# Second-norm rows turned in 32x32 blocks on VectorE for two of four superblocks, keys turned within a projection group, and a reordered VectorE queue

## The chip, the cores and the metric

One Trainium2 chip, one of its cores. The metric is the device time of one execution in microseconds, from the runs of a kernel on the chip; the median of the runs counts. TensorE multiplies matrices and turns (transposes) tiles through the identity matrix, VectorE and ScalarE work on rows and read the banks of PSUM, POOL (GpSimd) works beside them, and SyncE (SP) issues the DMAs.

## The reference

A decoder block over 2048 tokens of width 1024, float32, then a final norm:

```python
u = rmsnorm(h, ln1_g[l])
proj = u @ w_in[l]
a_q, a_f, a_i, a_g, b_q, b_k, b_v = jnp.split(proj, SPLITS, axis=-1)
y_a = hgrn2_mixer(a_q, a_f, a_i, a_g, lower_bounds[l], hgrn_norm_g[l])
y_b = swa_sink_attention(b_q, b_k, b_v, attn_sinks[l], attn_norm_g[l])
h = h + jnp.concatenate([y_a, y_b], axis=-1) @ w_out[l]
u = rmsnorm(h, ln2_g[l])
h = h + (jax.nn.silu(u @ w_gate[l]) * (u @ w_up[l])) @ w_down[l]
```

`hgrn2_mixer` is a gated linear recurrence with 4 heads of 128 keys and values, in chunks of 64 tokens: within a chunk masked products of decayed queries and keys, between chunks a state `S = decay * S + keys^T values`, and a norm per head. `swa_sink_attention` has 8 query heads of 64 on 2 key heads, a window of 128 tokens, a linear bias and a sink. The change touches the recurrence's turned keys and states, the turned probabilities of the attention, and the second `u`.

## The kernel before

**Stages.** The tokens are taken in four superblocks of 512 (`it` = 0 to 3, four row blocks of 128 tokens each). For each the kernel computes the mixers: first norm, projection, recurrence, attention, output projection (`slots`, then `out_b`). Then the feed-forward network runs on two pairs of superblocks (`ffn`, `down`), with seven instead of eight block products. Every product of two float32 matrices is made of three products of split operands, hi and lo.

**Slots.** The order of the mixers is written out by hand: each engine has its own function `slots(it)`, which goes through slots 0 to 26. Slots 0 to 21 each begin on TensorE with a `group`: 24 products that compute 128 columns of the projection for 512 tokens. Smaller steps hang on the slots by offsets. Head `a` of the recurrence begins at slot `F_SLOT[a]`, that is 4, 9, 14 and 18. From there its forget gate, queries, values and output gate are projected in slots +0 to +3, its keys are turned and its states updated at +4 (`UPDATE`), its output is made at +5 (`OUTPUT`, which reads the states `st`), and it is normalised and turned at +5 and +6. The sixteen steps of attention run one slot apart, from slot 2 on; a step's probabilities are turned on TensorE in slots 4 to 19, two steps at a time, and VectorE brings them out of PSUM with `unfold` (line 1892).

**Units.** Slots 22 to 25 and `out_b` compute the output projection. A weight pair of 1 MB (hi and lo) is a unit, 30 to a superblock: 22 groups, four units of the first half (22 to 25), four of the second (26 to 29, in `out_b`). From superblock 1 on SyncE loads unit n with `load_split` (line 642) as soon as TensorE has done with unit n - 3, into one of three places. In `out_b` TensorE turns the next superblock's x (`prep`, line 1011): row block 0 behind unit 26, block 1 behind unit 27, blocks 2 and 3 behind unit 28. Block 1 goes to the banks M2 and M3; those are free once VectorE's `add` (line 2088) has added the output projection in them to the rows of x, which SyncE loads again with `load_rows` (line 619).

**Turned keys.** POOL writes a head's decayed keys into `kstate`, which shares memory with `forget`. `key_turn` (line 1132) turns them on TensorE into bank X3, ScalarE copies them to `kst` (line 1415), `update` on TensorE (line 1141) multiplies them with the values, and `update` on VectorE (line 1953) makes eight states in a chain. TensorE reads these in the next slot (line 1148).

**The second norm.** A superblock's rows h are squared, scaled by VectorE (line 2162) and turned while the next superblock's mixers run, in slots 18 to 25 (`UT_SLOT` = 18): step j turns half of a row block with four transposes on TensorE (`u_turn`, line 1186) into bank X0, ScalarE copies the bank to a tile `u` (`u_out`, line 1469, semaphore `s_uev`), and SyncE stores it in DRAM as `u_scr` (`store_u`, line 661, semaphores `s_us`), for `ffn` to read. The last superblock's rows are turned within `ffn`.

**SyncE's queue** is one list, in `mixers(it)`. It waits at a DMA until that DMA may go, and all behind wait too. Stores of u stand between the loads of units:

```python
for c in range(4):
    for what, n in ((("u", 3), ("r", 0), ("r", 1), ("u", 4)), (("u", 5), ("r", 2), ("u", 6)),
                    (("u", 7), ("r", 3)), ())[c]:
        if what == "u":
            store_u(it - 1, n)
        elif not last or n >= 2:
            load_rows(it, n)
    load_split(it, OUT_B + c)
```

Stores 0, 1 and 2 stand behind the loads of units 22, 23 and 24.

## Time and profile before

| | us |
|---|---|
| median of 3 runs | 2169.05 (2166.82 to 2170.37) |
| the profiled execution's own time | 2167.59 |
| its span, first to last instruction | 2165.9 |
| TensorE busy | 2134.2 (99%) |
| VectorE busy | 1364.3 (63%) |
| ScalarE busy | 843.6 (39%) |
| POOL busy | 432.5 (20%) |

The mixers take the span up to some 900 us, with superblocks 1 and 2 from 246 to 459 us and from 459 to some 676 us; the rest is the feed-forward network. A row of the trace gives line, engine, operation and tile; L1186 is line 1186 of the kernel. Durations of matrix products overlap (they are pipelined), so the chain of work, which gives each piece the time that it adds, tells better what a product costs. The engines' busy shares are of one profiled execution.

### The profile page before, as it was taken

The numbers are of one execution on the slowest core, as the hardware profiler recorded it, in microseconds if no ns is written. First come the engines' busy times: TensorE is split into PE (matmuls) and PEld (weight loads), VectorE is DVE, ScalarE is ACT, GpSimd is POOL, SyncE is SP. The second block draws the span as 40 slices with busy tenths as digits, with TensorE's granted clock in tenths as the row PEclk, the third lists the DMA queues.
The fourth block names the chain that finished last, engine by engine and source line by source line (L and its number), as shares of the span: only waits on it lengthen the run. The fifth ranks groups of instructions, "written<-read, shape, count | busy, mean of one in ns | idle before, by whom it ended". The sixth has DMA issues, their size and how long they took to land.

```text
span 2165.9 us, 28872 instructions
## 1 busy us (share of the span) xinstructions
PE 2134.2 (99%) x10708; PEld 1778.9 (82%) x10708; DVE 1364.3 (63%) x2136; ACT 843.6 (39%) x1628; POOL 432.5 (20%) x403
## 2 busy tenths in 40 slices
PE   8999999999999999999999999999999999999998
PEld 7878888888888888788888887888888888888886
DVE  5886477547754776766566765568755556564556
ACT  5343342324232423444333333356433333333445
POOL 2342022102210221222233230000222233210000
PEclk9999999999999999999999999999999999999999
DMA  7666754664467437543355657887433323237666
GB/s 247 227 231 209 264 183 145 198 223 179 146 196 229 171 132 235 217 148 115 107 209 214 218 191 234 261 267 253 172 101 102 106 89 122 93 105 236 225 208 228
DMA packets 215740, 402.48 MB, mean 186 GB/s; under 512 B 16944, under 2 KB 100912, under 8 KB 211760
## 3 DMA queue, kind: packets, MB, share of 16 engines
q1 hardware_dynamic: 215600, 400.63, 54.6%
q8 instruction: 86, 1.41, 0.3%
q14 instruction: 54, 0.44, 0.1%
HBM read 292.04 MB, written 108.53 MB: 185 GB/s over the span
## 4 chain that ended last, share of the span: by engine, by line
PE 87%; DVE 5%; issue 4%; DMA 2%; ACT 1%; POOL 1%; SPq 0%; DVEq 0%; ACTq 0%; POOLq 0%
PE M L1282 10%; PE M L1284 10%; PE M L1283 10%; PE M L971 6%; PE M L973 6%; PE M L972 6%; PE M L1307 3%; PE M L1309 3%; PE M L1308 3%; PE X L1309 3%; PE X L1308 3%; PE X L1307 3%; PE X L1284 3%; PE X L1282 3%; PE X L1283 3%
## 5 line engine op out<-in xcount | busy, mean ns | idle before, releaser
L2292 DVE TENSOR_TENSOR ring_lo<-ring_raw,ring_hi 128x1024 fp32r<-128x1024 f32 x154 | 189.7, 1232 | 162.6 <-ACT ring_hi L1707 162.1
L1707 ACT ACTIVATE ring_hi<-ring_raw 128x1024 fp32r<-128x1024 f32 x154 | 163.3, 1061 | 230.4 <-DMA ring_raw<-a_scr 225.5
L1282 PE MATMUL M<-t_hi,wu_hi 128*128 128x512 f32 x616 | 240.2, 390 | 0.3 <-DVE wu_lo L2180 0.3
L1284 PE MATMUL M<-t_hi,wu_lo 128*128 128x512 f32 x616 | 239.9, 390 | 0.0
L1283 PE MATMUL M<-t_lo,wu_hi 128*128 128x512 f32 x616 | 239.7, 389 | 0.0
L971 PE MATMUL M<-uhi,split 128*128 128x512 f32 (+1 forms) x528 | 206.6, 391 | 2.9 <-DVE ulo L1843 2.9
L973 PE MATMUL M<-uhi,split 128*128 128x512 f32 (+1 forms) x528 | 202.9, 384 | 0.0
L972 PE MATMUL M<-ulo,split 128*128 128x512 f32 (+1 forms) x528 | 202.4, 383 | 0.0
L2180 DVE TENSOR_TENSOR wu_lo<-fraw,wu_hi 128x512 fp32r<-128x512 f32 x132 | 124.0, 948 | 123.3 <-ACT wu_hi L1649 122.9
L2557 POOL TENSOR_TENSOR fs<-fraw 128x512 f32<-128x512 f32 x43 | 61.0, 1418 | 415.8 <-DMA fraw<-in_w_gate_dram 208.5
L2477 POOL TENSOR_TENSOR pr<-pr,rd 128x256 f32<-128x256 f32 x64 | 44.6, 697 | 459.1 <-DVE rd L1854 459.1
L1282 PEld LDWEIGHTS M<-t_hi,wu_hi 128*128 128x128 f32 x616 | 115.6, 188 | 25.0 <-DVE wu_lo L2180 1.1
L1283 PEld LDWEIGHTS M<-t_lo,wu_hi 128*128 128x128 f32 x616 | 115.8, 188 | 24.1
L1284 PEld LDWEIGHTS M<-t_hi,wu_lo 128*128 128x128 f32 x616 | 115.6, 188 | 24.1
L2563 POOL TENSOR_TENSOR fraw<-fraw,fs 128x512 f32<-128x512 f32 x43 | 55.9, 1300 | 369.1 <-DVE wl_lo L2180 369.1
L1307 PE MATMUL M<-ring_hi 128*128 128x512 f32 x308 | 120.4, 391 | 2.3 <-DVE ring_lo L2292 2.3
L1308 PE MATMUL M<-ring_lo,ring_hi 128*128 128x512 f32 x308 | 119.9, 389 | 0.0
L1309 PE MATMUL M<-ring_hi,ring_lo 128*128 128x512 f32 x308 | 119.9, 389 | 0.0
L1307 PE MATMUL X<-ring_hi 128*128 128x512 f32 x308 | 119.8, 389 | 0.0
L1309 PE MATMUL X<-ring_hi,ring_lo 128*128 128x512 f32 x308 | 119.8, 389 | 0.0
L1308 PE MATMUL X<-ring_lo,ring_hi 128*128 128x512 f32 x308 | 119.8, 389 | 0.0
L971 PEld LDWEIGHTS M<-uhi,split 128*128 128x128 f32 x528 | 99.3, 188 | 23.9 <-issue 5.1
(312 smaller groups left out, 5012.6 us busy)
## 6 DMA issues: line engine op xcount, KB each, us to landing
split<-w_scr SPq DMA_DIRECT2D x60, 1024.0 KB, 5.6
ring_raw<-a_scr SPq DMA_DIRECT2D x154, 256.0 KB, 3.6
w_scr<-split SPq DMA_DIRECT2D x30, 1024.0 KB, 6.5
split_next<-w_scr SPq DMA_DIRECT2D x30, 1024.0 KB, 5.0
fraw<-in_w_gate_dram SPq DMA_DIRECT2D x44, 512.0 KB, 4.8
fraw<-in_w_up_dram SPq DMA_DIRECT2D x44, 512.0 KB, 4.8
a_scr<-au SPq DMA_DIRECT2D x88, 256.0 KB, 2.4
ring_raw<-t_scr SPq DMA_DIRECT2D x88, 256.0 KB, 3.0
```

Source lines behind the costliest of these rows:

```text
L971: mm(bank, whi[s][:, kb, :], hi, start=first, stop=False)
L972: mm(bank, whi[s][:, kb, :], lo, start=False, stop=False)
L973: return mm(bank, wlo[s][:, kb, :], hi, start=False, stop=last)
L1282: mm(bank[:, :], wh[:, k, :], hi[:, k, :], start=start and k == 0, stop=False, skip_group_check=True)
L1283: mm(bank[:, :], wh[:, k, :], lo[:, k, :], start=False, stop=False, skip_group_check=True)
L1284: last = mm(bank[:, :], wl[:, k, :], hi[:, k, :], start=False, stop=k == KH - 1, skip_group_check=True)
L1307: mm(bank[:, :], hi[:, 1, tokens], hi[:, 0, :], start=first, stop=False, skip_group_check=True)
L1308: mm(bank[:, :], hi[:, 1, tokens], lo[:, 0, :], start=False, stop=False, skip_group_check=True)
L1309: done = mm(bank[:, :], lo[:, 1, tokens], hi[:, 0, :], start=False, stop=last, skip_group_check=True)
L1707: A(hi[:, :, :], raw_r[:, :, :], ACT.Copy).then_inc(s_rowhi, 1)
L2180: V.tensor_tensor(wl[:, :, :], ffn_part(p, g, o), wh[:, :, :].bitcast(F32), ALU.subtract).then_inc(s_flo, 1)
L2292: V.tensor_tensor(lo[:, :, :], raw_r[:, :, :], hi[:, :, :].bitcast(F32), ALU.subtract).then_inc(s_rowlo, 1)
```

## The change

It does five things.

- `BY_BLOCKS = 2`: for superblocks 0 and 1, VectorE turns the scaled rows (`u_blocks`): one instruction transposes every 32x32 block of a 128x512 piece in place within the tile's grid, straight from h into the tile `u`. TensorE's `u_turn` and ScalarE's `u_out` remain for superblocks 2 and 3.
- Because the blocks are turned but not moved, `store_u` places them: for those superblocks each of the eight stores becomes 16 DMAs, each of 32 partitions x 4 x 32 elements (16 KB, in pieces of 128 bytes). Counts of `s_us` follow (`u_stored`), and loads that waited for TensorE's turns wait for `s_uev`.
- `key_turn` moves from behind the group of its slot into the group, between its fourth and fifth column block, for slots 8, 13 and 18.
- VectorE's state update of head 2, in slot 18, moves ahead of the scans of head 3.
- Two unfoldings move later: the first of slot 5 to that slot's end, that of slot 13 to the end of slot 14.

```diff
@@ constants, and in block_program
+UNFOLD_LATE = (5, 13)
+BY_BLOCKS = 2
+        def u_stored(it, times):
+            parts = [16 if i < BY_BLOCKS else 1 for i in range(NSB)]
+            return 16 * (2 * sum(parts[:it]) + times * parts[it])
@@ SyncE: load_rows, store_u
-                    sp.wait_ge(s_ftr, (it - 1) * 2 * TB + 2 * b + 2)
+                    sp.wait_ge(s_uev, (it - 1) * 2 * TB + 2 * b + 2)
...
-                sp.dma_start(u_scr[it, :, 4 * half:4 * half + 4, b * P:(b + 1) * P],
-                             u_tile(it, j)[:, :].rearrange("p (c t) -> p c t", c=4)).then_inc(s_us[j % 4], 16)
+                if it >= BY_BLOCKS:
+                    sp.dma_start(u_scr[it, :, 4 * half:4 * half + 4, b * P:(b + 1) * P],
+                                 u_tile(it, j)[:, :].rearrange("p (c t) -> p c t", c=4)).then_inc(s_us[j % 4], 16)
+                    return
+                for i in range(4):
+                    tokens = slice(b * P + 32 * i, b * P + 32 * i + 32)
+                    blocks = u_tile(it, j)[32 * i:32 * i + 32, :].rearrange("c (k m t) -> c k m t", k=4, m=4)
+                    for m in range(4):
+                        sp.dma_start(u_scr[it, 32 * m:32 * m + 32, 4 * half:4 * half + 4, tokens],
+                                     blocks[:, :, m, :]).then_inc(s_us[j % 4], 16)
@@ TensorE: group, slots, out_b
-            def group(it, slot):
+            def group(it, slot, head=None):
...
                 for k in range(KD):
+                    if head is not None and k == KD // 2:
+                        key_turn(it, head)
...
-                        group(it, slot)
+                        group(it, slot, head_at(slot, UPDATE))
...
-                    a = head_at(slot, UPDATE)
-                    if a is not None and slot != OUT_A:
-                        key_turn(it, a)
...
-                    if it and 0 <= slot - UT_SLOT < 2 * TB:
+                    if it > BY_BLOCKS and 0 <= slot - UT_SLOT < 2 * TB:
                         u_turn(it - 1, slot - UT_SLOT)
...
-                        if c == 0 and bank == 0 and it:
+                        if c == 0 and bank == 0 and it > BY_BLOCKS:
                             pe.wait_ge(s_uev, it * 2 * TB)
+                        elif c == 0 and bank == 0:
+                            pe.wait_ge(s_bias, (it + 1) * STEPS)
@@ ScalarE: slots
-                    if it and 0 <= slot - UT_SLOT < 2 * TB:
+                    if it > BY_BLOCKS and 0 <= slot - UT_SLOT < 2 * TB:
                         u_out(it - 1, slot - UT_SLOT)
@@ VectorE: head_group, slots, and a new step
                     dve.wait_ge(s_f, n + 1)
+                    if a == HEADS - 1:
+                        update(it, a - 1)
...
-                        unfold(it, i)
+                        if slot not in UNFOLD_LATE:
+                            unfold(it, i)
...
-                        if a is not None:
+                        if a is not None and (step is not update or slot != F_SLOT[-1]):
                             step(it, a)
+                    for late, i in ((5, 1), (14, 9)):
+                        if slot == late:
+                            unfold(it, i)
...
+                    if 0 < it <= BY_BLOCKS and 0 <= slot - UT_SLOT < 2 * TB:
+                        u_blocks(it - 1, slot - UT_SLOT)
...
+            def u_blocks(it, j):
+                b, half = divmod(j, 2)
+                dve.wait_ge(s_u, it * TB + b + 1)
+                if j >= 4:
+                    dve.wait_ge(s_us[j % 4], u_stored(it, 1))
+                else:
+                    dve.wait_ge(s_score, (it + 1) * STEPS + STEPS)
+                V.transpose(u_tile(it, j)[:, :], h_of(it)[b][:, half * T:(half + 1) * T]).then_inc(s_uev, 1)
```

What SyncE's queue holds from the load of unit 25 to that of unit 28, in superblock 1 (`split` and `split_next` are the places of weight pairs, `h` are the rows of x). Before:

```order
L642 DMA split<-w_scr 128x2x1024
L661 DMA u_scr<-u_152 128x4x128
L619 DMA h_71<-in_x_dram 128x1024
L619 DMA h_72<-in_x_dram 128x1024
L661 DMA u_scr<-u_149 128x4x128
L642 DMA split<-w_scr 128x2x1024
L661 DMA u_scr<-u_150 128x4x128
L619 DMA h_73<-in_x_dram 128x1024
L661 DMA u_scr<-u_151 128x4x128
L642 DMA split_next<-w_scr 128x2048
L661 DMA u_scr<-u_152 128x4x128
L619 DMA h_74<-in_x_dram 128x1024
```

With the change:

```order
L649 DMA split<-w_scr 128x2x1024
L676 DMA u_scr<-u_152 32x4x32 x16
L626 DMA h_71<-in_x_dram 128x1024
L626 DMA h_72<-in_x_dram 128x1024
L676 DMA u_scr<-u_149 32x4x32 x16
L649 DMA split<-w_scr 128x2x1024
L676 DMA u_scr<-u_150 32x4x32 x16
L626 DMA h_73<-in_x_dram 128x1024
L676 DMA u_scr<-u_151 32x4x32 x16
L649 DMA split_next<-w_scr 128x2048
L676 DMA u_scr<-u_152 32x4x32 x16
L626 DMA h_74<-in_x_dram 128x1024
```

The order is the same; 80 DMAs stand where 5 stood.

VectorE in slots 18 and 19 of superblock 1 (`forget` is the forget gate, `cum` the scans, `st` the states, `u` the new transposes). Before:

```order
L1900 TENSOR_SCALAR forget<-forget,f_mul,f_add 128x512
L1907 SCALAR_TENSOR_TENSOR cum_115<-forget,ones 128x64 x8
L1953 SCALAR_TENSOR_TENSOR st_138<-state,cum_114,X 128x128
L1953 SCALAR_TENSOR_TENSOR st_138<-st_138,cum_114,X 128x128 x3
L1953 SCALAR_TENSOR_TENSOR st_139<-st_138,cum_114,X 128x128
L1953 SCALAR_TENSOR_TENSOR st_139<-st_139,cum_114,X 128x128 x3
L1892 TENSOR_TENSOR pT_136<-X,keep 128x1024
```

With the change:

```order
L1916 TENSOR_SCALAR forget<-forget,f_mul,f_add 128x512
L1971 SCALAR_TENSOR_TENSOR st_138<-state,cum_114,X 128x128
L1971 SCALAR_TENSOR_TENSOR st_138<-st_138,cum_114,X 128x128 x3
L1971 SCALAR_TENSOR_TENSOR st_139<-st_138,cum_114,X 128x128
L1971 SCALAR_TENSOR_TENSOR st_139<-st_139,cum_114,X 128x128 x3
L1925 SCALAR_TENSOR_TENSOR cum_115<-forget,ones 128x64 x8
L2182 STREAM_TRANSPOSE u_149<-h_71 128x512
L1908 TENSOR_TENSOR pT_136<-X,keep 128x1024
```

The states stand ahead of the eight scans, and the first transpose behind them.

TensorE around slot 18 of superblock 1 (`M` is the group's bank, `forget` the keys, `kst` the turned keys). Before:

```order
L971 MATMUL M<-uhi,split_next 128x512
L972 MATMUL M<-ulo,split_next 128x512
L973 MATMUL M<-uhi,split_next 128x512
L1132 MATMUL X<-ident,forget 128x128 x4
L1141 MATMUL X<-iv,kst 128x128 x8
L1186 MATMUL X<-ident,h_71 128x128 x4
L971 MATMUL M<-uhi,split 128x512
```

With the change:

```order
L986 MATMUL M<-uhi,split_next 128x512
L987 MATMUL M<-ulo,split_next 128x512
L988 MATMUL M<-uhi,split_next 128x512
L1149 MATMUL X<-ident,forget 128x128 x4
L986 MATMUL M<-uhi,split_next 128x512
L987 MATMUL M<-ulo,split_next 128x512
L988 MATMUL M<-uhi,split_next 128x512
```

The turn of the keys has products of the group on both sides, twelve before it and twelve behind.

## Rows read from the trace of the kernel before

**Rows 1.** The page: busy time and share, and the granted clock in 40 slices.

```profile
PE 2134.2 (99%) x10708; PEld 1778.9 (82%) x10708; DVE 1364.3 (63%) x2136; ACT 843.6 (39%) x1628; POOL 432.5 (20%) x403
...
PEclk9999999999999999999999999999999999999999
```

**Rows 2.** Waits of TensorE: us in total, times, longest us.

```profile
PE X L1148 <- DVE st L1953: 5.7, 5, 1.8
...
PE X L1141 <- ACT kst L1415: 2.7, 4, 0.7
```

**Rows 3.** Order of time on TensorE: start, duration, in brackets the idle time before.

```profile
128.41 1.16 PE L1148 MATMUL X<-iv,amask 128*128 128x128 f32 x8 [1.79 <-DVE st L1953]
...
160.20 0.63 PE L1132 MATMUL X<-ident,forget 128*128 128x128 f32 x4 [0.44 <-ACT iv L1409]
161.51 1.16 PE L1141 MATMUL X<-iv,kst 64*128 64x128 f32 x16 [0.69 <-ACT kst L1415]
170.22 1.16 PE L1148 MATMUL X<-iv,amask 128*128 128x128 f32 x8 [1.44 <-DVE st L1953]
...
780.23 1.16 PE L1148 MATMUL X<-iv,amask 128*128 128x128 f32 x8 [0.83 <-DVE st L1953]
```

**Rows 4.** The chain, slots 20 and 21 of superblock 1: start, us, what.

```profile
395.77 0.58 PE X L1186 x4
...
404.00 0.44 PE X L1186 x4
```

**Rows 5.** Order of time on TensorE, products behind a turn of u.

```profile
379.24 0.48 PE L971 MATMUL M<-uhi,split 128*128 128x512 f32 x1
...
380.03 0.39 PE L971 MATMUL M<-uhi,split 128*128 128x512 f32 x1
```

**Rows 6.** VectorE's lines: count, busy us, mean ns, idle before.

```profile
L1892 DVE TENSOR_TENSOR pT<-X,keep 128x1024 int32<-128x1024 int32 x32 | 39.1, 1222 | 4.1 <-PE X L1087 4.1
...
L2032 DVE COPY oT<-M 128x512 f32<-128x512 f32 x16 | 11.0, 685 | 3.6 <-PE M L1099 3.6
```

**Rows 7.** SyncE's issues by line: ns min/median/max of one issue.

```profile
L642 SPq DMA_DIRECT2D split<-w_scr x60: 517/529/577, 241.2 to 873.2; - x60
L642 SPq DMA_DIRECT2D split_next<-w_scr x30: 319/326/351, 230.6 to 861.8; - x30
...
L661 SPq DMA_DIRECT2D u_scr<-u x16: 359/514/602, 385.6 to 645.7; - x16
...
L712 SPq DMA_DIRECT2D t_raw<-u_scr x32: 320/430/672, 811.6 to 1426.4; - x32
```

**Rows 8.** Order of time on SyncE's queue, from slot 22 of superblock 1.

```profile
411.00 0.59 SPq L661 DMA_DIRECT2D u_scr<-u  x1
411.65 1.54 SPq L619 DMA_DIRECT2D h<-in_x_dram  x2
...
428.85 1.25 SPq L619 DMA_DIRECT2D h<-in_x_dram  x1
```

**Rows 9.** The chain: second turn of superblock 2's x (eight transposes).

```profile
445.05 0.87 PE M L1011 x8
```

**Rows 10.** Order of time on VectorE: addition of row block 3.

```profile
437.24 0.69 DVE L2088 TENSOR_TENSOR h<-h,M 128x512 f32<-128x512 f32 x1 [1.99 <-DMA h<-in_x_dram]
```

**Rows 11.** The DMA issues by line: count, KB each, median us to landing.

```profile
h<-in_x_dram SPq DMA_DIRECT2D x14, 512.0 KB, 7.1
```

**Rows 12.** Two stretches: PE, PEld, DVE, ACT, POOL busy, clock, DMA share, GB/s.

```profile
385.00:393.00 8.00, 8.00 (x56) 6.78 (x55) 4.86 (x5) 3.27 (x12) 1.59 (x3) 1.00 0.57 166
...
427.00:433.00 6.00, 6.00 (x30) 4.96 (x29) 1.94 (x2) 3.08 (x6) 0.00 (x0) 1.00 1.02 330
```

**Rows 13.** The transfers from 9 to 14 us.

```profile
DMA packets 2911, 1.41 MB, mean 282 GB/s; under 512 B 1667, under 2 KB 2697, under 8 KB 2911
...
q1 hardware_dynamic: 2911, 1.41, 102.3%
```

**Rows 14.** The page's DMA queue: packets, MB, share of 16 engines.

```profile
q1 hardware_dynamic: 215600, 400.63, 54.6%
```

More of the change, by code:

```diff
@@ L364, in u_tile @@
             return (u_main, u_main, u_third, u_last)[it][j % 4]
+        def u_stored(it, times):
+            parts = [16 if i < BY_BLOCKS else 1 for i in range(NSB)]
+            return 16 * (2 * sum(parts[:it]) + times * parts[it])
         def wait_u_stored(eng, it, j=7):
             for n in range(4):
-                eng.wait_ge(s_us[n], 32 * it + 16 * ((j - n) // 4 + 1))
+                eng.wait_ge(s_us[n], u_stored(it, (j - n) // 4 + 1))
         M = [ctx.enter_context(nc.psum_tensor(f"M{i}", [P, T], F32)) for i in range(4)]
@@ L708, in load_operand @@
                 if p == 0 and o == B22:
-                    sp.wait_ge(s_ftr, (NSB - 2) * 2 * TB + 4)
+                    sp.wait_ge(s_uev, (NSB - 2) * 2 * TB + 4)
                     sp.wait_ge(s_u, (NSB - 1) * TB)
@@ L1460, in u_out @@
             def u_out(it, j):
-                act.wait_ge(s_ftr, it * 2 * TB + j + 1)
+                act.wait_ge(s_ftr, (it - BY_BLOCKS) * 2 * TB + j + 1)
                 if j >= 4:
-                    act.wait_ge(s_us[j % 4], 32 * it + 16)
+                    act.wait_ge(s_us[j % 4], u_stored(it, 1))
                 elif it == NSB - 1:
@@ L1528, in slots @@
                             for par in range(2):
-                                act.wait_ge(s_us[2 * p + par], 32 * (it - 1))
+                                act.wait_ge(s_us[2 * p + par], u_stored(it - 2, 2))
                         for par in range(2):
```

## The prediction

> **What bounds the kernel now.** I read the page first. TensorE is busy for 2134.2 of the 2165.9 us, VectorE for 63%, and the granted clock is at its full level all along [rows 1]. So time is won only by taking work or waits from TensorE, and lost only where a change makes TensorE wait. Next I read what TensorE waits for: little: 5.7 us for states made by VectorE, and 2.7 us for the turned keys that ScalarE copies out of PSUM [rows 2]. The order of time then gives the places [rows 3]: three of the waits shown are for states (1.79 us in slot 14 and 1.44 us in slot 19 of superblock 0; 0.83 us in slot 14 of superblock 3, and the same once in each of superblocks 1 and 2), and one for the turned keys, 0.69 us, which stands once in each superblock, in slot 18. Last I read SyncE's queue, because the change multiplies what it issues.
>
> **The change part by part**, each superblock's slots taken apart.
>
> *Turns of u leave TensorE.* A run of four costs 0.59 us on the chain, or 0.44 us where other fp32 work stands before it [rows 4]. Superblocks 0 and 1 have 16 such runs: ten at 0.59 and six at 0.44. Removed: 5.9 + 2.6 = 8.5 us. All of it lies on the path, since the chain runs through these very instructions.
>
> *Keys turned inside a group.* The copy that TensorE waited for now runs beside the second half of the group's products. That removes 4 x 0.69 = 2.8 us, and the 0.44 us wait for the turned values in superblock 0 [rows 3], which the first half covers. The turn itself costs what it cost. A product right behind a turn takes 0.48 us where others take 0.39 [rows 5]; the 12 moved turns each put one more such change into a group, at most 12 x 0.09 = 1.1 us lost, at least nothing. I take 1.1. POOL's part of the keys must be ready half a group earlier for a later head; it is made one or two slots ahead, so I cost that at nothing.
>
> *VectorE's order.* In slot 13 a 1.22 us unfolding [rows 6] stands before the states and now follows later. That covers the 0.83 us waits entirely (three of them, 2.5 us), and 1.2 of the 1.79 us. In slot 18 the states go ahead of eight scans, which covers 1.44 us. Together 5.1 us. What is late next is the scan of the last head, which VectorE reads itself in slot 19; it idles there for 3 of 8 us [rows 12], so nothing is lost.
>
> Gain so far: 8.5 + 2.8 + 0.4 - 1.1 + 5.1 = **15.7 us**. Should one of these covers fail and a wait of 0.7 to 1.8 us come back in some superblocks, it is about 13.
>
> *Sixteen transposes on VectorE.* No row shows one. The nearest are a copy of the same 128x512 tile out of PSUM, 0.69 us, and the unfolding of twice as many elements, 1.22 us [rows 6]. I take 0.7 us, between 0.5 and 1.3. They stand at the ends of slots 18 to 25, where no softmax is left; VectorE was busy for 4.86 of 8 us in one of them and 1.94 of 6 in another [rows 12], so even 1.3 us hides. The new waits on stored tiles (the fifth transpose waits for the first store) fall two slots behind the issue. Cost taken: nothing.
>
> *Stores in sixteen parts.* This is the term that decides. Each 256 KB store was one issue; now it is 16 of 16 KB, on the queue that also loads every weight pair. What an issue costs: 0.326 us in the median for 1 MB in one piece per partition, 0.529 us for 1 MB in two, 0.359 us at least for today's store, 0.430 us in the median for the 256 KB reads of u_scr [rows 7]. Size hardly enters, so parts of 16 KB are priced per issue. With 0.05 us between two issues (the store at 411.00 lasts 0.59 us and the next issue starts at 411.65, [rows 8]), one part takes between 0.37 us (0.32 + 0.05) and 0.58 us (0.53 + 0.05). Below that nothing in the trace lies, but the smallest DMA here has 128 rows and these have 32, so I do not exclude 0.2. I take i = **0.42 us**, today's store at its quickest, 0.36 us, plus the gap.
>
> Now follow SyncE from 411.00 us [rows 8], the point where it has just loaded the pair of unit 25. Until there, one store per slot of about 8 us (16i = 6.7 us) fits. From there five stores stand in the queue before the last x rows (row block 3): 80 issues. In between come three x loads and two weight loads, 2.7 us. The load of row block 3, at 428.85 us today, starts at 411.0 + 2.7 + 80i. It lands 7.1 us later [rows 11], and VectorE's addition takes 0.69 us [rows 10], so bank M3 is free at 421.5 + 80i. TensorE wants that bank for the turn of the next superblock's x, second half: today at 445.05 + 0.44 [rows 9], and 2.1 us earlier once the last four turns of u are gone. The addition was in fact already waiting for that load today, 1.99 us [rows 10], with some 8 us to spare before TensorE. The stall is therefore 421.5 + 80i - 443.4 = **80i - 21.9 us**. At 0.42 it is 11.7 us. The weight pair of unit 27, behind 64 of the parts, is late too, but by less, and this stall lies inside the other. The two superblocks are alike, so 23.4 us.
>
> **Sum**: 2167.6 (profiled execution; 2165.9 is its span) - 15.7 + 23.4 = 2175.3 us. The median of the runs is 1.5 us above the profiled execution, so I forecast **2176.8 us**. With i = 0.37 the stall is 7.7 us and the sum 2168.8; with 0.58 it is 24.5 us and the sum 2202.4.
>
> **The rivals.** A measurement of this kernel tells about 0.2% (4.3 us) from no change.
> 1. *Small parts issue quickly: faster.* If an issue's price follows its rows or descriptors, a part of 32 rows costs less than anything in the trace. The stall vanishes at i = 0.27, and then all 15.7 us stay: 2153.4 us. For it: the two issues of 1 MB differ by 0.2 us with nothing but their shape. Against: 256 KB and 1 MB in one piece cost the same at their quickest, 0.320 and 0.319 us [rows 7]. It decides from i below 0.34, where the time is 0.2% less than before. Chance 0.29.
> 2. *Gain and stall cancel.* i at the low end, 0.33 to 0.39 us: 2162 to 2172, about 2168. Chance 0.19, of which a third is still faster by 0.2%.
> 3. *The transfer engines choke on 128-byte pieces.* A store becomes 2048 packets of 128 bytes instead of 512 of 512, 128 for each of 16 engines. The trace bounds a packet: early on, when more than half of them were of a few bytes, 2911 packets kept the engines busy for 5 us, 28 ns each [rows 13]; over the run a packet takes 88 ns [rows 14] (54.6% of 16 x 2165.9 us over 215,600). So a store takes 3.6 to 11.3 us on the engines, against 6.7 us for its issues; and in the stretch from 427 to 433 us the engines are already full [rows 12]. At the middle, 58 ns and up, the packets set the pace instead, 7.4 us per store or more, with the x rows behind them: at 72 ns, i is in effect 0.58, and the time 2202. Chance 0.12.
>
> The Trainium skill ("DMA: Bandwidth & Descriptors", Specifications) speaks against the change here: it says that transfers of less than 512 B fall below line rate because the engine reads, modifies and writes. By that rule the packet of rival 3 would cost twice the 28 ns, 7.2 us a store, and the sum would be about 2182. No row here shows a 128-byte write.
>
> **How the numbers follow.** The main case (i from 0.39 to 0.5) has 0.40. Faster by over 0.2%: rival 1 and a third of rival 2, 0.35. Within: 0.13. Slower: 0.52. The range leaves out the far ends of rivals 1 and 3: 2150 to 2199. The likeliest case has its own range, 2172 to 2190.
>
> **What would show it.** The times between SyncE's issues of parts (0.42 us forecast); the issue of x row block 3 at about 445 us; a wait of VectorE's addition to h for that load, and behind it a wait of TensorE before the second turn of x, some 12 us, in superblocks 1 and 2 and not in 3; no waits for kst and st in slots 14, 18 and 19 but for some 0.6 us in superblock 0; transposes of about 0.7 us. If the parts come 0.3 us apart or less, the forecast is wrong and rival 1 holds. If they come 0.4 us apart and landings grow beyond 10 us, rival 3 holds. If TensorE waits in slots 18 to 25 for something of VectorE, the cover that I assumed is gone.

## The result, and the profile after

The change takes 2199.85 us (median of 4 runs, 2197.7 to 2202.3), the kernel before 2169.7 us on the same chip: ratio 1.0146, 95% interval 1.0134 to 1.0158. It is slower by 30 us, where 7 had been forecast, and lies 0.85 us above the range. The sign was right and the size was not. The experiments show why: the prediction took the loss by the stores too small and the gain by the rest too large, by 12 and 11 us.

The page of the change, against [rows 1]:

```profile
PE 2140.2 (97%) x10644; PEld 1778.0 (81%) x10644; DVE 1371.0 (62%) x2152; ACT 836.2 (38%) x1612; POOL 430.9 (20%) x403
...
PEclk9999999989998999999999999999999999999999
```

Sixty-four instructions fewer on TensorE, sixteen more on VectorE, and yet TensorE is busy for 6 us longer, while the granted clock falls in two places, one in superblock 1 and one in superblock 2. What TensorE waits for, against [rows 2]:

```profile
PE X L994 <- DMA split_next<-w_scr: 16.1, 2, 8.2
PE X L994 <- DMA split<-w_scr: 10.3, 4, 4.4
PE X L1149 <- ACT iv L1425: 7.5, 5, 3.1
...
PE X L1165 <- DVE st L1971: 0.2, 1, 0.2
```

One kind is new, 26.4 us for weight pairs that are being loaded, and one has grown, from 0.4 to 7.5 us, that for the turned values. Of the waits for states (5.7 us before) 0.2 us are left, and of those for the turned keys (2.7) nothing. SyncE's queue from slot 21 of superblock 1 on shows where the first kind comes from, against [rows 8]:

```profile
396.87 7.73 SPq L676 DMA_DIRECT2D u_scr<-u  x16
404.70 0.38 SPq L649 DMA_DIRECT2D split_next<-w_scr  x1
405.12 8.36 SPq L676 DMA_DIRECT2D u_scr<-u  x16
413.58 0.53 SPq L649 DMA_DIRECT2D split<-w_scr  x1
...
431.63 0.53 SPq L649 DMA_DIRECT2D split<-w_scr  x1
...
448.11 0.38 SPq L649 DMA_DIRECT2D split_next<-w_scr  x1
448.53 7.61 SPq L676 DMA_DIRECT2D u_scr<-u  x16
456.18 0.43 SPq L626 DMA_DIRECT2D h<-in_x_dram  x1
```

A store of sixteen parts takes between 7.6 and 8.5 us, 0.48 us for each part in the quicker ones. With the weight pair between two stores that is 8.3 to 9.0 us, more than the slot of 8 us that it has, so SyncE is behind before the x rows come. The pair at 431.63 is unit 26's, the one at 448.11 unit 27's; x row block 3, issued at 428.85 us before [rows 8], goes out at 456.18. On TensorE:

```profile
437.12 0.69 PE L994 MATMUL X<-split,yhi 128*128 128x512 f32 x1 [4.36 <-DMA split<-w_scr]
444.29 1.04 PE L1026 MATMUL M<-ident,os 128*128 128x128 f32 x8
453.15 0.80 PE L994 MATMUL X<-split_next,yhi 128*128 128x512 f32 x1 [7.83 <-DMA split_next<-w_scr]
460.88 1.03 PE L1026 MATMUL M<-ident,os 128*128 128x128 f32 x8
```

TensorE waits at the first product of unit 26 and of unit 27, both times for the weights. The second turn of x (L1026 at 460.88, before at 445.05 [rows 9]) has no wait in front of it. VectorE's addition of row block 3 did wait, for 15.51 us:

```profile
459.93 0.69 DVE L2112 TENSOR_TENSOR h<-h,M 128x512 f32<-128x512 f32 x1 [15.51 <-DMA h<-in_x_dram]
```

It ended at 460.6, just before TensorE came for the bank. Had the weight pairs been in time, this would have been the next gate.

The waits also made the products behind them slower. The same four rows before:

```profile
433.11 0.39 PE L979 MATMUL X<-split,yhi 128*128 128x512 f32 x1
...
438.55 1.03 PE L1011 MATMUL M<-ident,os 128*128 128x128 f32 x8
439.34 0.48 PE L979 MATMUL X<-split_next,yhi 128*128 128x512 f32 x1
...
444.88 1.03 PE L1011 MATMUL M<-ident,os 128*128 128x128 f32 x8
```

From the first product of unit 26 to the turn behind its 24 products 5.4 us passed before and 7.2 us pass now, for unit 27 5.5 us and 7.7 us. The clock behind the two waits:

```profile
437.00:440.00 3.00, 2.88 (x7) 2.33 (x8) 0.00 (x0) 0.00 (x0) 0.00 (x0) 0.54 0.25 39
440.00:443.00 3.00, 3.00 (x13) 2.40 (x13) 0.00 (x0) 0.00 (x0) 0.00 (x0) 0.89 0.62 173
...
450.00:453.00 3.00, 0.00 (x0) 0.00 (x0) 0.00 (x0) 0.00 (x0) 0.00 (x0) 0.50 0.96 331
453.00:456.00 3.00, 2.85 (x7) 2.27 (x8) 0.00 (x0) 0.00 (x0) 0.00 (x0) 0.50 0.30 46
456.00:459.00 3.00, 3.00 (x11) 2.40 (x10) 0.00 (x0) 0.00 (x0) 0.00 (x0) 0.71 0.62 158
```

The granted clock is the number behind the five busy times (0.54 in the first row). 0.50 is the 1.2 GHz level. At full clock a product starts 0.227 us after the one before it, 13 in 3 us; in the stretch from 453 to 456 us there are 7.

### The profile page after: what moved, and what is told of

The parts are those of the page before. It is cut to its first block, busy times and chain, and to the rows that moved or that the text cites. A ratio compares the mean times of both kernels' runs of the same rounds, so it can differ in the third digit from the quotient of the medians.

```text
span 2196.0 us, 28967 instructions
## 1 busy us (share of the span) xinstructions
PE 2140.2 (97%) x10644; PEld 1778.0 (81%) x10644; DVE 1371.0 (62%) x2152; ACT 836.2 (38%) x1612; POOL 430.9 (20%) x403
## 4 chain that ended last, share of the span: by engine, by line
PE 79%; DVE 6%; SPq 6%; issue 5%; DMA 2%; ACT 1%; POOL 1%; DVEq 0%; ACTq 0%; POOLq 0%
PE M L1300 10%; PE M L1298 10%; PE M L1299 10%; SPq L676 5%; PE M L986 5%; PE M L988 5%; PE M L987 5%; PE M L1323 3%; PE M L1325 3%; PE M L1324 3%; PE X L1325 3%; PE X L1323 3%; PE X L1324 3%; PE X L1300 3%; PE X L1299 3%
```

## The experiments

Seventeen kernels ran, in five groups. Every difference below is the ratio to the kernel before, on the same chip, times 2169 us, with its 95% interval.

### Which part costs what

`key_turn_alone`: only the key turns move into the groups.

```diff
+                    if head is not None and k == KD // 2:
+                        key_turn(it, head)
...
-                    if a is not None and slot != OUT_A:
-                        key_turn(it, a)
```

> The kernel before with the key turn moved into the group, and nothing else of the change. Theory A (the turn now stands half a group earlier and waits for ScalarE's copy of the values, which stands behind the softmax of that slot): slower by 6 to 8 us, about 2176; waits of TensorE for iv of some 7 us in all, in slots 13 and 18, no waits for kst, and slot 8 of superblock 0 1.6 us longer. Theory B (the prediction): faster by 2.1 us, 2167, no new wait.

Measured: 2175.36 us, +6.7 us (4.6 to 8.9), as theory A had it.

`order_alone`: only VectorE's order (two unfoldings later, the states of the last head ahead of its scans).

> The kernel before with VectorE's two reorderings alone (states of head 2 ahead of the scans, two unfoldings later). Theory A (the waits for st go and nothing takes their place): faster by 5 to 6 us, about 2164. Theory B (the gain seen behind slots 14 and 19 is only time that the late key turn had cost): no change.

Measured: 2166.3 us, -3.0 us (-5.2 to -1.1), between the two theories.

`blocks_alone`: only the blocks and their stores in parts; the other two parts undone.

> The kernel before with the block transposes and the stores in 16 parts alone. Theory A (SyncE's issues at 0.475 us, not 0.42, are late from the first store on; the weight pairs of units 26 and 27 come late and TensorE's clock falls while it waits): slower by 28 to 31 us, about 2199, of it 14 to 15 us in each of superblocks 1 and 2. Theory B (a good part of the loss comes from VectorE's new work next to the other edits): slower by less than 20 us.

Measured: 2198.91 us, +29.7 us (25.6 to 33.8), with 28.8 us of waits for weight pairs. Theory A holds: the loss needs neither of the other two parts.

So the key turn, forecast as a gain of 2.1 us, is a loss. The trace of the change shows the mechanism in slot 18 of superblock 1:

```profile
375.39 0.40 ACT L1457 ACTIVATE pr<-pr,nm 128x128 f32<-128x128 f32 x1 [4.27 <-DVE nms L1898]
...
376.27 0.58 ACT L1425 ACTIVATE iv<-X 128x512 f32<-128x512 f32 x1
376.99 0.63 PE L1149 MATMUL X<-ident,forget 128*128 128x128 f32 x4 [1.04 <-ACT iv L1425]
```

The key turn writes the bank from which ScalarE copies the turned values (iv). That copy stands in ScalarE's order behind its exponentials, which wait for VectorE's maxima (nms). Before, TensorE had a whole group's products to do until then; turned after half of them it comes 2.7 us earlier (12 products of 0.227 us from start to start) and waits. In slot 18 of superblock 0 the wait is 3.14 us instead of 0.44 [rows 3].

The same wait, 3.15 us in slot 18 of superblock 0 of `key_turn_alone`, had another sequel there. In that kernel the clock of the six microseconds around the turn was 0.59, in the change 1.00 (first and second row, each from 162 to 168 us):

```profile
162.00:168.00 6.00, 3.79 (x11) 3.23 (x12) 3.14 (x6) 2.05 (x7) 1.18 (x2) 0.59 0.72 252
```

```profile
162.00:168.00 6.00, 5.46 (x37) 4.40 (x38) 1.92 (x6) 2.54 (x4) 1.44 (x2) 1.00 0.94 343
```

Counted from the start of the slot's group, the product that uses the turned keys (`X<-iv,kst`) was 4.6 us later than before in this one slot with the key turns alone, and 2.0 us later within the change. This is no difference between the two kernels as such: `change_whole` and `change_loads_first`, below, have the change's key turns and the same wait (3.12 and 3.15 us), and their clock in these six microseconds was 0.72. So the clock fell behind this wait in three of four profiled executions. What decided it, no run shows.

### What the relief of TensorE is worth, and what the whole change would be without its stores

`blocks_whole` and `change_whole`: each tile of blocks is stored in one DMA, the former with the blocks alone, the latter with all three parts. Both leave out the placing of the blocks: what lies in `u_scr` is not u transposed, so only their time is of use.

```diff
-                for i in range(4):
...
-                    for m in range(4):
-                        sp.dma_start(u_scr[it, 32 * m:32 * m + 32, 4 * half:4 * half + 4, tokens],
-                                     blocks[:, :, m, :]).then_inc(s_us[j % 4], 16)
+                sp.dma_start(u_scr[it, :, 4 * half:4 * half + 4, b * P:(b + 1) * P],
+                             u_tile(it, j)[:, :].rearrange("p (c t) -> p c t", c=4)).then_inc(s_us[j % 4], 16)
```

> VectorE's blocks, stored whole in one DMA as before, so that SyncE's queue is as before (left out: the placing of the blocks, so what lies in u_scr is not u transposed). Neither the order on VectorE nor the key turns are changed. It measures what TensorE gains by losing 64 transposes, without the price of the stores. Theory A, from the event times of the earlier runs (the gap between the run with blocks alone and the kernel before shrinks by 2.2 us between slot 18 and the last turn of h, in each of two superblocks): 2169.7 - 4.4 = 2165 us, between 2162 and 2167. Theory B, the prediction's term (16 runs at 0.59 and 0.44 us leave the path whole): 2169.7 - 8.5 = 2161 us. No wait for split or split_next in either.

Measured: 2162.02 us, -6.3 us (-8.9 to -3.7), between the two theories. Theory A's gain was too low because its 2.2 us were counted in the order of time between slot 18 and the last turn of a head's output, and two of the eight runs of four come behind that. At the second turn of x TensorE had gained 3.1 us on the kernel before in each of the two superblocks, 0.38 us for each run.

> The whole change with its three parts, but each tile of u stored whole in one DMA (left out: the placing of the blocks). It tests the prediction's 'gain so far' of 15.7 us at one stroke. Theory A, by the event times (stall of 16.6 us in each of two superblocks taken from the change, some 1.5 us of it that the ffn stage made good given back): 2199.9 - 33.2 + 1.5 = 2168 us, between 2165 and 2170, with TensorE waiting some 7 us for iv as in the change. Theory B, the prediction: 2169.7 - 15.7 = 2154 us.

Measured: 2164.48 us, -4.8 us (-6.9 to -2.8). Theory A was 3.5 us too high, and the prediction's gain of 15.7 us is refuted even with the stores in one piece. The change proper took 35.4 us more (2199.85 - 2164.48): this is the whole price of the stores in parts. `blocks_alone` and `blocks_whole` give the same, 29.7 + 6.3 = 36.0 us.

Why a run of four is worth 0.38 us and not 0.59, TensorE's order of time shows, before and in `blocks_whole`:

```profile
387.26 0.66 PE L1186 MATMUL X<-ident,h 128*128 128x128 f32 x4
387.67 0.48 PE L971 MATMUL M<-uhi,split 128*128 128x512 f32 x1
387.98 0.39 PE L972 MATMUL M<-ulo,split 128*128 128x512 f32 x1
```

```profile
388.10 0.50 PE L982 MATMUL M<-uhi,split 128*128 128x512 f32 x1
388.44 0.40 PE L983 MATMUL M<-ulo,split 128*128 128x512 f32 x1
```

From the start of the run to the second product behind it pass 0.72 us; without the run, from the first product to the second, 0.34 us. The difference is 0.38 us. The duration printed beside a group (0.66 us) reaches over the start of what follows, and the first product of a group starts slowly with or without a turn ahead of it.

### Is it the issues, the pieces, or the transfer engines?

`sixteen_issues`, `wide32` and `wide128`: the kernel before, its tiles turned on TensorE, each stored in 16 DMAs of 16 KB cut three ways.

```diff
+                for i in range(16 if it < 2 else 1):
+                    n = 8 if it < 2 else P
+                    rows = slice(i * n, (i + 1) * n)
+                    sp.dma_start(u_scr[it, rows, 4 * half:4 * half + 4, b * P:(b + 1) * P],
+                                 u_tile(it, j)[rows, :].rearrange("p (c t) -> p c t", c=4)).then_inc(s_us[j % 4], 16)
```

> The kernel before, with TensorE's turns, but each store of u of superblocks 0 and 1 issued as 16 DMAs of 8 partitions, whose pieces stay 512 bytes. It tells the number of issues apart from the size of the pieces. Theory A (issues alone set the pace): the issues come 0.475 us apart and the time is that of the blocks alone plus the 6 to 8 us that the turns cost, 2204 to 2208. Theory B (the 128-byte pieces make SyncE or the transfers slow): below 2190.

Measured: 2177.88 us, +8.2 us (5.0 to 11.5). Theory A is refuted, and the number is on the side of theory B, the pieces. But the parts here differ from the change's in two things, the pieces and the 8 partitions instead of 32. The next two take these apart.

> The kernel before with its turned tiles stored in 16 DMAs of 32 partitions x one piece of 512 bytes, 32 pieces each (the run with 8 partitions x four pieces of 512 bytes, 32 pieces too, had its issues 0.357 us apart and took 2177.9 us; the change, 32 partitions x four pieces of 128 bytes, 128 pieces, 0.475 us apart). Theory A (the price follows the number of pieces): 0.36 us apart, about 2178 us. Theory B (it follows the number of partitions): 0.42 us or more apart, over 2185 us. Theory C (it follows the number of dimensions, one less here): 0.33 us or less apart, below 2175 us.

Measured: 2199.0 us, +30.4 us (25.8 to 34.7).

> The kernel before with its turned tiles stored in 16 DMAs of 128 partitions x one piece of 128 bytes, 128 pieces each. Theory A (pieces): 0.475 us apart, a stall as in the change, about 2202 us. Theory B (partitions): over 0.5 us apart, over 2205 us. Theory C (dimensions): 0.33 us or less apart, below 2175 us.

Measured: 2203.86 us, +34.1 us (30.8 to 37.3).

One store on SyncE's queue, in slot 21 of superblock 1, in `sixteen_issues`, `wide32` and `wide128`:

```profile
395.47 5.75 SPq L669 DMA_DIRECT2D u_scr<-u  x16
```

```profile
395.39 7.60 SPq L670 DMA_DIRECT2D u_scr<-u  x16
```

```profile
396.60 7.72 SPq L670 DMA_DIRECT2D u_scr<-u  x16
```

| 16 DMAs of 16 KB each | piece | us for 16 | time lost |
|---|---|---|---|
| 8 partitions x 4 pieces | 512 B | 5.75 | 8.2 |
| 32 partitions x 1 piece | 512 B | 7.60 | 30.4 |
| 32 partitions x 4 pieces (the change) | 128 B | 7.73 | 35.4 |
| 128 partitions x 1 piece | 128 B | 7.72 | 34.1 |

The time lost is against the kernel before, for the change against `change_whole`. The price of an issue does not follow the pieces: 8 partitions in 32 pieces cost 0.36 us, 32 partitions in 32 pieces 0.475 us, and 128 partitions in 128 pieces hardly more, 0.48. (Of the three theories of `wide32` B held; of those of `wide128` A, with a price that is the same as with 32 partitions; what grows between 8 and 32 partitions, and where, was not tried.) Pieces of 512 bytes at the change's pitch lose nearly what pieces of 128 bytes lose, so the transfer engines' work on small pieces is not the cause. A part lands in 2.3 us in the median in `wide32` and in 2.4 us in the change.

The last column also shows how steep the loss is. In `sixteen_issues` the eight stores of superblock 1 take 45.3 us of SyncE and those of superblock 2 47.1, in `wide32` 62.6 and 61.6 (five of the sixteen stores take 8.0 to 8.8 us there): 17 and 15 us more, for which a superblock loses 11.1 us more.

### Where in the queue the parts stand

`blocks_two_queues` and `order_two_queues`: ScalarE issues eight of a tile's sixteen parts, one slot behind the transposes; the latter with VectorE's order as in the change, both with the key turns as before.

```diff
-                for i in range(4):
+                for i in range(2):
...
+            def store_u_half(it, j):
+                b, half = divmod(j, 2)
+                act.wait_ge(s_uev, it * 2 * TB + j + 1)
+                for i in range(2, 4):
...
+                        act.dma_start(u_scr[it, 32 * m:32 * m + 32, 4 * half:4 * half + 4, tokens],
+                                      blocks[:, :, m, :]).then_inc(s_us[j % 4], 16)
```

> Blocks alone, with the same 16 DMAs of the same shapes, but SyncE issues eight of them and ScalarE the other eight, one slot behind the transposes. The bytes, the pieces and the transfer engines' work are those of blocks_alone (2198.9 us). Theory A (the time of the issues on SyncE's queue is the cause): SyncE spends 8 x 0.475 = 3.8 us on a store, ScalarE as much per slot, of which it is busy for 1.7 to 3.6 of 8 us, so both fit; no wait for split or split_next, and the time is within 2 us of blocks_whole, about 2165 us. Theory B (the transfer engines choke on pieces of 128 bytes): the weight pairs land late as before, and the time stays over 2185 us. Theory C (ScalarE becomes what is waited for): no wait for a split, but TensorE waits for iv, uhi or the squares in slots 19 to 26, 1 to 3 us per superblock, 2167 to 2171 us.

Measured: 2167.18 us, -0.9 us (-2.8 to 1.1). These are the parts of `blocks_alone`, issued from two queues. Of its 28.8 us of waits for weight pairs 3.6 are left, all for unit 27's, and with the other 25 us most of the slow clock behind them went too: 30.6 us in all. That refutes theory B. Theory A is right in the cause and not in its number: the time is 5.2 us above `blocks_whole`, of which the 3.6 us are these waits. TensorE has no new wait for ScalarE, so it is not theory C. A part lands later than before, in 4.1 us in the median on SyncE's queue against 2.4 in the change, and still the time comes back.

> As blocks_two_queues, with VectorE's order of the change added and the key turns left where they were. If the parts add up: the time of blocks_two_queues less the 2 to 3 us of order_alone, about 2162.5 us, the fastest kernel of this study; if VectorE's later unfoldings and its transposes get in each other's way, no faster than blocks_two_queues.

Measured: 2164.26 us, -5.0 us (-6.9 to -2.8), 2.9 us below `blocks_two_queues`: VectorE's order adds what it gives alone.

`change_loads_first` and `order_loads_first`: all parts on SyncE, but behind the loads. The latter has the key turns as before.

```diff
+                    if n > OUT_A and blocks:
+                        store_u(it - 1, n - OUT_A - 1)
...
+                    for what, n in (((("r", 0), ("r", 1)), (("r", 2),), (("r", 3),), ()) if blocks else
...
                     load_split(it, OUT_B + c)
+                    if blocks:
+                        store_u(it - 1, 3 + c)
...
                     load_split(it + 1, 1)
+                    if blocks:
+                        store_u(it - 1, 7)
```

> The whole change, correct placing, all 256 parts still on SyncE; only the order of SyncE's queue in superblocks 1 and 2 is another: each weight pair and each x row block is loaded ahead of the store that stood before it, and the last store stands behind the next superblock's first two loads. Bytes, pieces, issues and their time are those of the change (2199.9 us). Theory A (the loads were late because parts stood in front of them; by the issue times of the change, 8 x 8 us of parts and 8 us of loads fit between slot 20 and the next superblock's first group): the pair of unit 27 is issued near 424 us, row block 3 near 433 us, no wait for split or split_next over 1 us; the time is within 3 us of change_whole, 2164 to 2168 us. Theory B (the parts as such burden the transfer engines or the queue as a whole): later loads are now late instead, or stores hold back the transposes of tiles 5 to 8; over 2180 us.

Measured: 2179.9 us, +9.8 us (6.7 to 12.8).

> As change_loads_first, with the key turns left where they were before the change: what the experiments so far say is the best of the parts. By the parts: relief of TensorE -6.3 (blocks_whole), order on VectorE -2 to -3, no stall: 2169.7 - 9 = 2160.5 us, between 2158 and 2163. If TensorE still waits some 2 us per superblock for a weight pair as with two queues, 2164 us.

Measured: 2172.95 us, +3.7 us (1.5 to 5.6). Neither theory held as written. Of the 35 us, 20 (2199.85 - 2179.9) were lost by the order alone, with not one issue fewer. The rest stayed, since the queue was also full as such. VectorE and SyncE in `change_loads_first`:

```profile
436.51 0.71 DVE L2190 STREAM_TRANSPOSE u<-h 128x512 f32<-128x512 f32 x1 [4.02 <-DMA u_scr<-u]
```

```profile
435.68 0.37 SPq L649 DMA_DIRECT2D split_next<-w_scr  x1
436.09 7.77 SPq L676 DMA_DIRECT2D u_scr<-u  x16
443.90 0.44 SPq L626 DMA_DIRECT2D h<-in_x_dram  x1
444.44 0.53 SPq L649 DMA_DIRECT2D split<-w_scr  x1
...
462.33 0.43 SPq L649 DMA_DIRECT2D split_next<-w_scr  x1
```

Unit 27's pair goes out at 435.68 instead of 448.11, row block 3 at 443.90 instead of 456.18, and unit 28's pair at 444.44. TensorE now waits for unit 28's pair (1.6 us here), for row block 3 (0.6 us), and most for the next superblock's first pair (2.3 us), which goes out at 462.33. A store put off also holds back a transpose, by 4.0 us, but the transpose was done at 437.2, and row block 3's load, which needs it, stood behind the sixteen parts of 436.09 for 6.7 us more. So the queue is the cause, and not the transpose.

`two_queues_load_27`: as `order_two_queues`, with one load moved.

```diff
+                    if c == 1 and 0 < it <= BY_BLOCKS:
+                        load_split(it, OUT_B + 1)
                     for what, n in ((("u", 3), ("r", 0), ("r", 1), ("u", 4)), (("u", 5), ("r", 2), ("u", 6)),
```

> As order_two_queues (2164.3 us; TensorE waited 1.9 us for the pair of unit 27 in each of two superblocks, its load having been issued at 432.5 us against 426.5 us before), with one thing moved: SyncE loads the pair of unit 27 ahead of the stores of tiles 6 and 7 (tile numbers from 1). Theory A (place in the queue is all that is left of the stall): the load is issued before 426 us, no wait for a split, and the 3.9 us with some slow clock behind them come back: 2160 us, between 2158 and 2162. Theory B (two queues issuing small parts slow the transfers themselves): the pair still lands too late and the time stays at 2164 us.

Measured: 2166.44 us, -0.9 us (-3.7 to 2.0): no better. The wait for unit 27 is gone, as theory A had it, but two others stand in its place, one of them the gate that the prediction had named:

```profile
PE X L997 <- DMA split<-w_scr: 2.8, 2, 1.6
...
PE M L1029 <- DVE h L2130: 2.1, 2, 1.3
```

Row block 3 and unit 28's pair were issued at 436.89 and 437.43, behind the stores of two tiles.

`three_superblocks` has the blocks in the third superblock too (`BY_BLOCKS = 3`).

> As two_queues_load_27, with the blocks used for the third superblock too, whose u is turned in superblock 3, where SyncE also loads the ffn's first operands. If TensorE's relief is worth the same there (3.1 us) and nothing is late: 3 us less than two_queues_load_27. If the operand loads behind the parts are late, or ScalarE, which has the splitting of the operands there, is: no gain or a loss of up to 10 us, seen as waits at the start of the ffn.

Measured: 2173.98 us, +5.2 us (3.3 to 7.4). The relief came (TensorE gained 3.1 us on `two_queues_load_27` over the eight runs of superblock 3), and more was lost behind it. The parts there stand in one queue with the ffn's operands and the last weight pairs, and one of these came late:

```profile
882.35 0.79 PE L997 MATMUL X<-split,yhi 128*128 128x512 f32 x1 [7.58 <-DMA split<-w_scr]
```

### The key turn later, and all parts mended

`key_turn_late`: as `key_turn_alone`, with the turn before the last of the group's eight k.

```diff
-                    if head is not None and k == KD // 2:
+                    if head is not None and k == KD - 1:
```

> Only the key turns of the change, but before the last of the group's eight products of k instead of the fifth (2.04 us later). Theory A (TensorE reaches the turn before ScalarE has copied the turned values, which stand behind its exponentials; the run with the turn in the middle waited 7.3 us for iv, 3.1 once, 1.3 once and 1.04 three times): the waits of 1.04 and 1.3 us vanish and the longest shrinks to 1.1 us, so that the time is about that of the kernel before, within 2 us (2168 to 2171 us), with the 0.69 us waits for the turned keys either gone or partly back. Theory B (the turn inside a group costs by itself, in slower products around it, some 0.5 us each): 2173 us or more, as with the turn in the middle (2175.4 us).

Measured: 2165.93 us, -2.8 us (-5.0 to -0.9). The turn inside the group costs nothing by itself. What TensorE waits for:

```profile
PE X L1151 <- DVE st L1953: 4.0, 5, 1.7
...
PE X L1135 <- ACT iv L1409: 1.1, 1, 1.1
```

The waits for kst are gone, as the prediction said, and of the waits for iv one is left. What this part of the change was meant for works; its place after half the products undid it.

`order_key_late`: VectorE's order and the late key turns.

> VectorE's order of the change, and the key turns inside their groups, but before the last of the eight products of k. The turns of u and their stores are left as before. By the parts: order_alone -2 to -3, key_turn_late -2.8 (interval -4.9 to -0.9), each taking away waits that the other leaves (states; turned keys): 2169 - 5.5 = 2163.5 us, between 2161 and 2166, with neither st nor kst among TensorE's waits but for 0.7 us. If the two give back each other's gain (both end at POOL's keys), no faster than 2166 us.

Measured: 2162.52 us, -6.1 us (-8.5 to -3.9). The two add up (-3.0 and -2.8 alone).

`all_mended`: the change with late key turns, two queues, and the loads of unit 27, row block 3 and unit 28 ahead of the stores they stood behind.

```diff
-                    if head is not None and k == KD // 2:
+                    if head is not None and k == KD - 1:
...
+                    if c == 1 and blocks:
+                        load_split(it, OUT_B + 1)
...
-                                    (("u", 7), ("r", 3)), ())[c]:
+                                    (("r", 3),) if blocks else (("u", 7), ("r", 3)), ())[c]:
...
+                    if c == 2 and blocks:
+                        store_u(it - 1, 7)
```

> All three parts of the change, mended where the runs say it lost: key turns before the last product of k; the 16 stores of a tile issued half by SyncE and half by ScalarE; and in SyncE's queue the pair of unit 27 ahead of the stores of tiles 6 and 7, row block 3 and the pair of unit 28 ahead of the store of tile 8 (in two_queues_load_27 these two were issued at 436.9 and 437.4 us and TensorE then waited 0.8 us for row block 3's addition and 1.6 us for the pair). Now they go out some 4 us earlier, near 433 us. By the parts: -5.5 for order and late key turns, -6.3 for the turns of u: 2169 - 11.8 = 2157 us, between 2154 and 2161, and no wait for a split or for h over 0.3 us. If the gate only moves on to the next load again (unit 29 or the next superblock's first), 2161 to 2163 us.

Measured: 2155.88 us against 2168.4 us, ratio 0.9943 (0.9930 to 0.9955), -12.4 us (-15.2 to -9.8). It beats both kernels, and by what the parts give alone: -6.1 (`order_key_late`) and -6.3 (`blocks_whole`). SyncE's queue, from unit 27's pair on:

```profile
423.17 0.34 SPq L649 DMA_DIRECT2D split_next<-w_scr  x1
...
429.41 3.82 SPq L676 DMA_DIRECT2D u_scr<-u  x8
433.27 0.44 SPq L626 DMA_DIRECT2D h<-in_x_dram  x1
433.82 0.53 SPq L649 DMA_DIRECT2D split<-w_scr  x1
```

Row block 3 and unit 28's pair go out 3.6 us earlier than in `two_queues_load_27`, and of waits for weights 0.3 us are left:

```profile
PE X L1000 <- DMA split<-w_scr: 0.3, 1, 0.3
```

## Why the prediction was right or wrong

- **What bounds the kernel**: right. TensorE is the bound, and time was lost only where the change made it wait or run at a lower clock.
- ***Turns of u leave TensorE*, 8.5 us**: mis-sized. It measured 6.3 us, by the order of time 16 x 0.38 = 6.1. The step took the time of a group on the chain (0.58 and 0.44 us [rows 4]), which the section on the profile before calls the better guide to what a product costs. It is not: the distance between starts was to be taken, and the same distance without the run subtracted. The order of time on TensorE had both numbers.
- ***Keys turned inside a group*, -2.1 us**: wrong in sign, +6.7 us alone. The step asked whether POOL's keys would be ready half a group earlier, and whether the turned values' wait would be covered; it did not ask when ScalarE's copy of them ends, though [rows 3] has a wait of 0.44 us on just that copy at the old, later place. A wait that stands there already becomes longer when its consumer moves ahead. It was read the wrong way round: the first half of the group does not cover it, the second half had done so. Put before the last of the eight products of k the step is right, -2.8 us.
- ***VectorE's order*, -5.1 us**: mis-sized, it measured -3.0 us (-5.2 to -1.1). The waits for states vanished nearly as forecast (5.7 to 0.7 us in `order_alone`), but of the 1.1 us that slot 14 won in each of superblocks 1 to 3, 0.3 was given back by slot 16 and 0.5 in slot 17, there at the products with POOL's keys, for which TensorE now waited six times instead of three (3.4 us in all, 2.8 before). "What is late next" named the last head's scan; it was POOL's keys.
- **Gain of 15.7 us**: 4.8 us (2.8 to 6.9) in `change_whole`. This is 11 of the 23 us by which the forecast missed.
- ***Sixteen transposes on VectorE*, nothing**: right, 0.70 us each, with no wait of TensorE for them:

```profile
L2182 DVE STREAM_TRANSPOSE u<-h 128x512 f32<-128x512 f32 x16 | 11.2, 701 | 0.0
```

- ***Stores in sixteen parts*, 23.4 us**: mis-sized, 35.4 us, the other 12 of the 23. The step that failed first is i = 0.42, "today's store at its quickest" plus the gap: an issue took 0.48 us, in the range given. That broke the sentence "one store per slot of about 8 us (16i = 6.7 us) fits": 7.7 us and a load are 8.3. With 0.48 the formula 80i - 21.9 gives 16.5 us per superblock, against the measured 17.7, and with the 4.8 us of `change_whole` for the gain the prediction's sum would be 2167.6 - 4.8 + 33.0 + 1.5 = 2197.3 us. So the formula's size was nearly right, but in part by luck, since its mechanism was not: the named gate, row block 3, was never waited for by TensorE in the change. The pair of unit 27, "late too, but by less", and that of unit 26, which the prediction did not name, held it first (12.2 us in superblock 1, with 0.7 us more at the next pair). In both superblocks these waits are 26.4 of the 35.4 us. Of the other 9.0 us 8.1 (3.9 and 4.2) are what the products of units 26 and 27 took longer, mostly at the lower clock; that term was missing from the sum. That row block 3 was close behind was right, as `two_queues_load_27` shows.
- **Rival 1** (small parts issue quickly) was wrong: only the cut into 8 partitions is cheaper, and not cheap enough. **Rival 2** fell with it. **Rival 3** (transfer engines and 128-byte pieces) gave 2202 us, nearest to the result. The nearness is luck: its mechanism is refuted by `wide32`, which loses 30.4 us with no piece under 512 bytes, and by `all_mended`, which gains with all the 128-byte pieces in place. The rule of the Trainium skill ("DMA: Bandwidth & Descriptors", Specifications) that smaller transfers than 512 B are read, modified and written had no visible price here: the parts landed in 2.4 us in the median, those of 512-byte pieces in 2.3. Only the 5 us between `wide32` and the change could lie in it, and the interval of `wide32` alone is 9 us wide.

## What to carry to other kernels

Price an instruction that leaves a pipelined engine by the distance between the starts of its neighbours, with and without it, and never by the duration that stands beside it. Before a step is moved ahead on one engine, look up for each of its inputs when it is made, and in whose order; an existing wait at the old place, however small, says that there is no room. When one DMA becomes many, set the time of the issues against the slot with the loads included, and put urgent loads ahead of the stores that nobody waits for; after each such mending look for the next gate, since here three loads had to be moved, one after the other, before the whole gain showed.

## What the runs showed of the hardware

- On SyncE a DMA of 16 KB takes 0.36 us from issue to issue with 8 partitions and 0.475 to 0.48 us with 32 or 128 partitions, whether its pieces have 128 or 512 bytes (one store of each kernel divided by 16; about every third store with 32 or 128 partitions takes 0.5 us and more for a part). ScalarE's queue is no quicker: one issue has 454 ns in the median in `blocks_two_queues`, against 432 on SyncE in the change, and 24 issues take 13.1 us in `all_mended`.
- The clock behind a wait: after 4.36 us of waiting TensorE's granted clock was 0.54 over the next 3 us, after 7.83 us it was 0.50, then 0.71 over the next 3 us, and full from 459 us on, 6 us after the work had begun. Of four waits of 3.1 us at the same place in four kernels, behind three it fell (0.59, 0.72 and 0.72 over six microseconds), and behind one it stayed at 1.00.
- A 128x512 transposition of float32 in blocks of 32 takes VectorE 0.70 us, as long as a copy of such a tile out of PSUM [rows 6].
